# Attention by pairs of heads in alternating halves of TensorE's array, eight score buffers, division on VectorE

## The chip, the cores and the metric

The kernel runs on one core of a Trainium2 chip. Its engines work side by side and meet at semaphores: TensorE (PE, with its weight loads PEld), VectorE (DVE), ScalarE (ACT), GpSimd (POOL), and SyncE (SP), which issues most transfers. The metric is the device time of one execution in microseconds (us); lower is better.

## What is computed

Two transformer-like blocks over 512 tokens of width 1024. The first block (mixer, cross attention and feed-forward, twice) is not touched. The second block projects the tokens, runs an RWKV-7 state over eight heads, an attention over eight other heads, gates both and projects them out. The attention, of 8 heads of width 64, is what the change touches:

```python
def chunk_band_attention(q, k, v, q_g, k_g, rel_bias):
    ...
    s = jnp.einsum('bhnqd,bhnkd->bhnqk', qc, kb).astype(jnp.float32) * (HEAD_DIM ** -0.5)
    ...
    bias = rel_bias[:, rel_idx].astype(jnp.float32)
    ...
    s = s + bias[None, :, None]
    s = jnp.where(valid[None, None, :, None, :], s, -1e30)
    p = jax.nn.softmax(s, axis=-1).astype(v.dtype)
    o = jnp.einsum('bhnqk,bhnkd->bhnqd', p, vb)
    return o.reshape(b_, N_ATT_HEADS, s_, HEAD_DIM).transpose(0, 2, 1, 3).reshape(b_, s_, D_ATT)

# second_block
        y_a = chunk_band_attention(q, ka, va, q_norm_g[l], k_norm_g[l], rel_bias[l])
        y = jnp.concatenate([y_r * jax.nn.silu(g_r), y_a * jax.nn.silu(g_a)], axis=-1)
        x = x + gate[:, None, :] * (y @ w_out[l])
```

## The kernel before

**Products of weights.** Every large product is made of three matmuls of split operands (`mm3`, L324 to L326). ACT makes a weight chunk's high part (L298), VectorE its low part (L308), SP loads the chunks into three or four places in turn. `hi_to` and `lo_to` are where ACT and VectorE make the chunks due by then.

**Attention in tiles.** A tile k is one head h = k // 4 and 128 queries q = k % 4; causal, so it has 128 (q+1) keys. For each pair of tiles (k, k+1) of one head: TensorE makes the scores (`scores`, L1472; K is 64, so a matmul uses one half of the array's rows: heads with even number the first, odd ones the second); VectorE scales and adds the bias into a buffer `Sb[k % 4]` (L1534, L1535), takes the maximum of each tile (L1539), negates both (L1541), waits for ACT's exponentials of this pair (L1505) and takes the reciprocals of their sums (L1543); POOL divides (L1567); TensorE transposes the 128x128 pieces (`turned`, L1482); ACT copies them into `PTa[h % 2]` (L1513). When a head's four tiles are there, TensorE multiplies by the values (`values`, L1493, output in 64 of the 128 partitions of a bank), and VectorE gates (L1552). An fp32 matmul is two matmul instructions with a weight load each in the profile.

**The order.** `att_turns` writes the order out by hand, the same for each engine: in the step of pair n, first the values of a finished head, then `turned` for pair n-4, a yield, the scores of pair n, a yield. The yields interleave this with the dense products. `gemm_n` and `gemm_c` call `side()` after every six matmuls, through the stages `av` (attention's values) and `ag` (its gate); `late` is the generator of attention. The first scores come at the 15th of the 16 sides of `av`. The 16 sides of `ag` take attention up to `turned` of tiles 14 and 15. `closing` runs beside it in `ag`: it makes the diagonal for the output gate (VectorE L2348, TensorE L2327) and the gated RWKV rows (L2354, L2356).

**The tail.** Then `second_pe` and its like of the other engines run a loop of 18 turns. Each takes one step of attention; turns 1 to 8 add on TensorE one first part of the output product (`out_part_pe`, tokens t, row tiles 0 to 3, which hold the RWKV rows). Part (0,0) waits for the low half of those rows (`split_act` L2363, `split_dve` L2367, in turns 0 to 3 after that turn's step of attention). In turn 10, after the step of attention, ACT and VectorE make three weight chunks (`hi_to`, `lo_to`, n_out2 + 5). After the loop, attention's rows are split (L2439, L2457) and the output product goes on: parts 2 and 3 of each token tile, then the second half of the columns.

**The banks.** There are eight PSUM banks in a queue (`Banks`): `take` gives the one given back longest ago, and its new user waits until the old content was read (`vacant`). In the tail the output product holds four, so attention has the other four in turn.

## Time and profile before

| what | value |
| --- | --- |
| median of 3 runs | 1930.52 us (1925.89 to 1934.94) |
| the profiled execution's own time | 1928.67 us |
| its span, first to last instruction | 1926.8 us |
| TensorE busy | 1851.0 us, 96% |
| VectorE busy | 1028.7 us, 53% |
| ACT busy | 648.9 us, 34% |
| POOL busy | 172.2 us, 9% |
| mean granted TensorE clock | 0.983 of full |

The page's slices show TensorE's share of busy time and its granted clock along the span; the groups of instructions show what one instruction costs by shape; the chain that ended last shows which engine was waited for. Busy times of pipelined matmuls overlap, so the cost of a group on TensorE is read from the start of its first instruction to the start of the next group's first. The attention runs from 1775 to 1888 us of the span.

### The profile page before, as it was taken

How to read it: one execution, taken by the hardware profiler on the slowest of the kernel's cores; microseconds unless marked ns; L12 is line 12 of the kernel's file. 1: busy time of each engine (PE TensorE's matmuls, PEld its weight loads, DVE VectorE, ACT ScalarE, POOL GpSimd, SP SyncE). 2: the span in 40 equal slices, each digit the busy share in tenths (PEclk: the TensorE clock that was granted, in tenths of full speed). 3: DMA queues.
4: the chain of work that ended last, by engine and by line, in shares of the span. 5: the costliest groups of instructions: out<-in, count | busy, mean ns of one | idle time of the engine just before them, and what ended most of it. 6: DMA issues, size and time to landing. Idle time of an engine off the chain costs nothing.

```text
span 1926.8 us, 27348 instructions
## 1 busy us (share of the span) xinstructions
PE 1851.0 (96%) x11475; PEld 1529.8 (79%) x11475; DVE 1028.7 (53%) x1440; ACT 648.9 (34%) x999; POOL 172.2 (9%) x190
## 2 busy tenths in 40 slices
PE   7999999999999999999999999999989899998978
PEld 7879868888888898889868888878867787776546
DVE  4467347444454564446336556654566655445653
ACT  4332442323334322232432332334346232333441
POOL 3101001000000010001001000000020211111330
PEclk9999999999999999999999999999999999999998
DMA  8323323333323324332333545423232211114111
GB/s 269 113 88 109 99 66 99 120 93 94 98 88 121 98 90 119 98 110 99 99 105 122 155 149 164 143 88 99 77 109 61 59 57 35 46 35 143 41 37 44
DMA packets 145257, 189.65 MB, mean 98 GB/s; under 512 B 7688, under 2 KB 94980, under 8 KB 144240
## 3 DMA queue, kind: packets, MB, share of 16 engines
q1 hardware_dynamic: 139088, 168.32, 28.0%
q0 software_dynamic: 3488, 10.07, 1.6%
q10 hardware_dynamic: 2560, 9.53, 1.3%
q8 instruction: 91, 1.49, 0.3%
q14 instruction: 30, 0.25, 0.0%
HBM read 181.58 MB, written 6.30 MB: 98 GB/s over the span
## 4 chain that ended last, share of the span: by engine, by line
PE 87%; DVE 6%; issue 2%; ACT 2%; DMA 1%; POOL 1%; POOLq 0%; ACTq 0%; DVEq 0%
PE ps L324 25%; PE ps L325 24%; PE ps L326 24%; PE ps L2039 2%; PE ps L932 1%; PE ps L908 1%; PE ps L2025 1%; DVE WL L308 1%; PE ps L1472 1%; PE ps L2000 1%; ACT WH L298 1%; DMA RAW<-ab_w_in 1%; PE ps L509 1%; PE ps L2160 1%; PE ps L1493 1%
## 5 line engine op out<-in xcount | busy, mean ns | idle before, releaser
L308 DVE TENSOR_TENSOR WL<-RAW,WH 128x1024 fp32r<-128x1024 f32 x289 | 356.6, 1247 | 526.2 <-ACT WH L298 525.5
L324 PE MATMUL ps<-XH,WH 128*128 128x512 f32 (+1 forms) x1416 | 525.5, 371 | 3.9 <-DVE XL L522 3.5
L326 PE MATMUL ps<-XH,WL 128*128 128x512 f32 (+1 forms) x1416 | 519.2, 367 | 0.0
L325 PE MATMUL ps<-XL,WH 128*128 128x512 f32 (+1 forms) x1416 | 519.2, 367 | 0.0
L298 ACT ACTIVATE WH<-RAW 128x1024 fp32r<-128x1024 f32 x289 | 301.6, 1057 | 609.8 <-PE ps L326 577.9
L324 PE MATMUL ps<-WH,XH 128*128 128x512 f32 x800 | 322.4, 403 | 11.8 <-issue 4.2
L325 PE MATMUL ps<-WL,XH 128*128 128x512 f32 x800 | 315.4, 394 | 0.0
L326 PE MATMUL ps<-WH,XL 128*128 128x512 f32 x800 | 314.9, 394 | 0.0
L324 PEld LDWEIGHTS ps<-XH,WH 128*128 128x128 f32 x1416 | 268.8, 190 | 55.5 <-issue 9.3
L326 PEld LDWEIGHTS ps<-XH,WL 128*128 128x128 f32 x1416 | 268.5, 190 | 43.8
L325 PEld LDWEIGHTS ps<-XL,WH 128*128 128x128 f32 x1416 | 268.9, 190 | 41.5 <-issue 0.5
L324 PEld LDWEIGHTS ps<-WH,XH 128*128 128x128 f32 x800 | 152.2, 190 | 50.2 <-issue 9.2
L326 PEld LDWEIGHTS ps<-WH,XL 128*128 128x128 f32 x800 | 152.4, 191 | 32.6
L325 PEld LDWEIGHTS ps<-WL,XH 128*128 128x128 f32 x800 | 152.6, 191 | 30.1 <-issue 0.5
L648 POOL TENSOR_SCALAR SM<-SM 128x1 f32<-128x1 f32 x28 | 34.3, 1226 | 1201.0 <-DVE SM L636 1200.7
L516 ACT ACTIVATE XH<-ps 128x512 fp32r<-128x512 f32 x48 | 25.2, 604 | 142.3 <-PE ps L509 142.3
L1135 ACT ACTIVATE SCR<-SCR,VEC 128x512 f32<-128x512 f32 x44 | 31.9, 724 | 113.1 <-DVE SCR L1166 113.1
L1197 DVE TENSOR_TENSOR XL<-BIG,XH 128x512 fp32r<-128x512 f32 x88 | 56.1, 685 | 1.4 <-ACT XH L1189 1.4
L1189 ACT ACTIVATE XH<-BIG 128x512 fp32r<-128x512 f32 x88 | 49.4, 616 | 2.3 <-PE ps L326 2.3
L1169 DVE TENSOR_TENSOR BIG<-SCR,ps 128x512 f32<-128x512 f32 x44 | 30.3, 688 | 34.8 <-ACT SCR L1135 34.8
L2075 ACT ACTIVATE SCR<-ps 128x512 f32<-128x512 f32 x32 | 19.1, 597 | 85.8 <-PE ps L2039 85.8
L1567 POOL TENSOR_SCALAR LATE<-LATE,SM 128x128 f32<-128x128 f32 (+3 forms) x32 | 38.0, 1199 | 79.7 <-DVE SM L1543 79.7
(332 smaller groups left out, 1960.3 us busy)
## 6 DMA issues: line engine op xcount, KB each, us to landing
RAW<-ffn_w_up SPq DMA_DIRECT2D x176, 256.0 KB, 3.2
RAW<-ffn_w_down SPq DMA_DIRECT2D x44, 512.0 KB, 3.6
RAW<-w_in SPq DMA_DIRECT2D x33, 512.0 KB, 3.9
RAW<-xa_wkv SPq DMA_DIRECT2D x32, 512.0 KB, 4.0
RAW<-c_w_in SPq DMA_DIRECT2D x24, 512.0 KB, 3.7
LATE<-w_ada SPq DMA_DIRECT2D x24, 512.0 KB, 4.9
RAW<-xa_wq SPq DMA_DIRECT2D x16, 512.0 KB, 5.5
RAW<-xa_wo SPq DMA_DIRECT2D x16, 512.0 KB, 3.7
```

The costliest lines, as they stand in the source:

```text
L298: e.activation(halves_of(i)[0][:, :, 0:w], raw(i)[:, :, 0:w], ACT.Copy).then_inc(*w_hi.up(i))
L308: e.tensor_tensor(wl[:, :, 0:w], raw(i)[:, :, 0:w], wh[:, :, 0:w].bitcast(F), ALU.subtract).then_inc(*w_lo.up(i))
L324: e.matmul(o, lh, rh, start=start, stop=False)
L325: e.matmul(o, lh, rl, start=False, stop=False)
L326: return e.matmul(o, ll, rh, start=False, stop=stop)
L648: e.tensor_scalar(vr[:, t:t + 1], mv[:, t, 1:2], 1e-5, None, ALU.add).then_inc(*ln_g.up((n, t, "eps")))
L1135: e.activation(gc[i], gc[i], ACT.Gelu_apprx_tanh, bias=vec(f"fcb{l}", j)).then_inc(*ffn_a.up(("gelu", l, j)))
L1169: e.tensor_tensor(hT[:, j, :], c, ps.tile((("up", l, nb), i))[:, :], ALU.mult).then_inc(*ps.empties((("up", l, nb), i), ffn_v, ("h", l, j)))
L1189: e.activation(XH[:, kt % 8, :], hT[:, kt, :], ACT.Copy).then_inc(*x_hi.up(("h", l, j, kt)))
L1197: e.tensor_tensor(XL[:, kt % 8, :], hT[:, kt, :], XH[:, kt % 8, :].bitcast(F), ALU.subtract).then_inc(*x_lo.up(("h", l, j, kt)))
L1567: e.tensor_scalar(s, s, asum[:, n % 8 + j:n % 8 + j + 1], None, ALU.mult).then_inc(*at_g.up(k))
L2039: r = e.matmul(o, lhs[pps[cp], h, :], rhs[pps[cp], h, :], start=True, stop=True)
```

## The change

- Tiles are numbered anew (`att_of`): eight tiles k make a pair of heads; k % 2 is the head of the pair, k % 8 // 2 the queries q. A pair of tiles (n, n+1) is now two heads with the same q and the same number of keys.
- `scores` on TensorE cuts the keys in two and issues head a, head b, head a, head b, so that matmuls alternate between the halves of the array's rows. `values` runs over a pair of heads, alternating the halves of the array's columns, into one whole bank.
- There are eight score buffers, the four new ones in GB, which is free by then. `turned` comes for pair n-6, and `values` and the loop of the tail move with it: 20 turns instead of 18. The turns of the output parts and of `hi_to` and `lo_to` (10) stay.
- VectorE takes the maximum of both tiles in one instruction, with the negation in it, and a new step `normed` for pair n-2 after the scores of pair n: reciprocals, then the division of both tiles. POOL's part goes. The gating is one product of 128 partitions for each pair of heads.

```diff
@@ -1369,7 +1369,7 @@
     qTa, kTa = v4(B[4]), v4(L[3])
     xr = XR[:, :, :].rearrange("p a b -> p (a b)")
     PTa = [v4(xr[:, 2048 * i:2048 * i + 2048]) for i in range(2)]
-    Sb = [L[1][:, 512 * i:512 * i + 512] for i in range(4)]
+    Sb = [(L[1] if i < 4 else GB)[:, 512 * (i % 4):512 * (i % 4) + 512] for i in range(8)]
@@ -1441,134 +1441,138 @@
...
-    def att_turns(scores, turned, values):
+    def att_of(k):
+
+        return 2 * (k // 8) + k % 2, k % 8 // 2
+
+    def att_turns(scores, normed, turned, values):
 
         ready = []
-        for n in range(0, 36, 2):
-            for h in ready:
-                values(h)
+        for n in range(0, 38, 2):
+            for j in ready:
+                values(j)
             ready = []
-            for k in (n - 4, n - 3):
-                if k >= 0:
-                    turned(k)
-                    if k % 4 == 3:
-                        ready.append(k // 4)
+            if n >= 6:
+                turned(n - 6)
+                turned(n - 5)
+                if n % 8 == 4:
+                    ready.append(n // 8 - 1)
             yield
             if n < 32:
                 scores(n)
-            yield
-        for h in ready:
-            values(h)
+            if 2 <= n < 34:
+                normed(n - 2)
+            yield
+        for j in ready:
+            values(j)
+
+    def nothing(*args):
+        pass
 
     def att_pe_run(e):
         def scores(n):
-            h = n // 4
+            q, nk = att_of(n)[1], 64 * (att_of(n)[1] + 1)
             for k in (n, n + 1):
-                q, nk = k % 4, 128 * (k % 4 + 1)
-                b = ps.take(("as", k))
+                ps.take(("as", k))
                 for w in ps.vacant(("as", k)):
                     e.wait_ge(*w)
-                e.wait_ge(*at_v.at(("qk", 1, 3)))
-                e.matmul(b[:, 0:nk], qTa[halves(h), h // 2, 128 * q:128 * q + 128], kTa[halves(h), h // 2, 0:nk],
-                         start=True, stop=True).then_inc(*at_pe.up(("as", k)))
+            e.wait_ge(*at_v.at(("qk", 1, 3)))
+            for c in range(2):
+                for k in (n, n + 1):
+                    h = att_of(k)[0]
+                    r = e.matmul(ps.tile(("as", k))[:, nk * c:nk * c + nk], qTa[halves(h), h // 2, 128 * q:128 * q + 128],
+                                 kTa[halves(h), h // 2, nk * c:nk * c + nk], start=True, stop=True)
+                    if c:
+                        r.then_inc(*at_pe.up(("as", k)))
             ps.back(("as", n), ("as", n + 1))
 
         def turned(k):
             b = ps.take(("ap", k))
             for w in ps.vacant(("ap", k)):
                 e.wait_ge(*w)
-            e.wait_ge(*at_g.at(k))
-            for m in range(k % 4 + 1):
-                r = e.transpose(b[:, 128 * m:128 * m + 128], Sb[k % 4][:, 128 * m:128 * m + 128], ident)
+            e.wait_ge(*at_v.at(("p", k)))
+            for m in range(att_of(k)[1] + 1):
+                r = e.transpose(b[:, 128 * m:128 * m + 128], Sb[k % 8][:, 128 * m:128 * m + 128], ident)
             r.then_inc(*at_pe.up(("ap", k)))
             ps.back(("ap", k))
 
-        def values(h):
-            b = ps.take(("av", h))
-            for w in ps.vacant(("av", h)):
+        def values(j):
+            b = ps.take(("av", j))
+            for w in ps.vacant(("av", j)):
                 e.wait_ge(*w)
-            e.wait_ge(*at_a.at(("ap", 4 * h + 3)))
+            e.wait_ge(*at_a.at(("ap", 8 * j + 7)))
             e.wait_ge(*p2_a.at(("qkv", 2, 3)))
             for m in range(4):
-                r = e.matmul(b[halves(h), 128 * m:512], va[m][:, 64 * h:64 * h + 64], PTa[h % 2][:, m, 128 * m:512],
-                             start=m == 0, stop=m == 3)
-            r.then_inc(*at_pe.up(("av", h)))
-            ps.back(("av", h))
-        yield from att_turns(scores, turned, values)
+                for h in (2 * j, 2 * j + 1):
+                    r = e.matmul(b[halves(h), 128 * m:512], va[m][:, 64 * h:64 * h + 64], PTa[h % 2][:, m, 128 * m:512],
+                                 start=m == 0, stop=m == 3)
+            r.then_inc(*at_pe.up(("av", j)))
+            ps.back(("av", j))
+        yield from att_turns(scores, nothing, turned, values)
 
     def att_act_run(e):
         def scores(n):
             i = n % 8
             e.wait_ge(*at_v.at(("max", n)))
             for j, k in enumerate((n, n + 1)):
-                nk = 128 * (k % 4 + 1)
-                e.activation(Sb[k % 4][:, 0:nk], Sb[k % 4][:, 0:nk], ACT.Exp, bias=am[:, i + j:i + j + 1],
+                s = Sb[k % 8][:, 0:128 * (att_of(k)[1] + 1)]
+                e.activation(s, s, ACT.Exp, bias=am[:, i + j:i + j + 1],
                              accum_out=asum[:, i + j:i + j + 1]).then_inc(*at_a.up(("e", k)))
 
         def turned(k):
-            q, h = k % 4, k // 4
+            h, q = att_of(k)
             e.wait_ge(*at_pe.at(("ap", k)))
-            if h >= 2:
-                e.wait_ge(*at_pe.at(("av", h - 2)))
+            if k >= 8:
+                e.wait_ge(*at_pe.at(("av", k // 8 - 1)))
             e.activation(PTa[h % 2][:, 0:q + 1, 128 * q:128 * q + 128],
                          ps.tile(("ap", k))[:, 0:128 * (q + 1)].rearrange("p (m n) -> p m n", n=128),
                          ACT.Copy).then_inc(*ps.empties(("ap", k), at_a, ("ap", k)))
-
-        def values(h):
-            pass
-        yield from att_turns(scores, turned, values)
+        yield from att_turns(scores, nothing, turned, nothing)
 
     def att_dve_run(e):
         def scores(n):
-            h, i = n // 4, n % 8
+            i = n % 8
             for k in (n, n + 1):
-                nk = 128 * (k % 4 + 1)
-                lo, s, b = max(0, nk - 256), Sb[k % 4], ps.tile(("as", k))
+                h, q = att_of(k)
+                nk = 128 * (q + 1)
+                lo, s, b = max(0, nk - 256), Sb[k % 8], ps.tile(("as", k))
                 e.wait_ge(*at_pe.at(("as", k)))
                 if k < 4:
                     e.wait_ge(*p2_g.at("bias"))
                     e.wait_ge(*st_pe.at(("y", 7)))
+                elif k < 8:
+                    e.wait_ge(*st_v.at(("y", 7)))
                 else:
-                    e.wait_ge(*at_pe.at(("ap", k - 4)))
+                    e.wait_ge(*at_pe.at(("ap", k - 8)))
                 if lo:
                     e.tensor_scalar(s[:, 0:lo], b[:, 0:lo], 0.125, bias(h, 0, 1), ALU.mult, ALU.add).then_inc(*at_v.up())
                 e.scalar_tensor_tensor(out=s[:, lo:nk], in0=b[:, lo:nk], scalar=0.125, in1=bias(h, 256 - (nk - lo), 256),
                                        op0=ALU.mult, op1=ALU.add).then_inc(*ps.empties(("as", k), at_v, ("s", k)))
-            for j, k in enumerate((n, n + 1)):
-                e.wait_ge(*at_v.at(("s", k)))
-                e.tensor_reduce(am[:, i + j:i + j + 1], Sb[k % 4][:, 0:128 * (k % 4 + 1)], AX.X, ALU.max).then_inc(*at_v.up())
-            e.wait_ge(*latest["V"])
-            e.tensor_scalar(am[:, i:i + 2], am[:, i:i + 2], -1.0, None, ALU.mult).then_inc(*at_v.up(("max", n)))
+            s2 = (GB if n % 8 >= 4 else L[1]).rearrange("p (k m) -> p k m", k=4)[:, n % 4:n % 4 + 2, 0:128 * (att_of(n)[1] + 1)]
+            e.wait_ge(*at_v.at(("s", n + 1)))
+            e.tensor_reduce(am[:, i:i + 2], s2, AX.X, ALU.max, negate=True).then_inc(*at_v.up(("max", n)))
+
+        def normed(n):
+            i = n % 8
             e.wait_ge(*at_a.at(("e", n + 1)))
             e.reciprocal(asum[:, i:i + 2], asum[:, i:i + 2]).then_inc(*at_v.up(("sum", n)))
-
-        def turned(k):
-            pass
-
-        def values(h):
-            b, p = ps.tile(("av", h)), halves(h)
-            e.wait_ge(*at_pe.at(("av", h)))
-            e.wait_ge(*p2_v.at(("ag", h // 2)))
-            e.scalar_tensor_tensor(out=sga[h // 2][p, :], in0=sga[h // 2][p, :], scalar=0.5, in1=b[p, :], op0=ALU.mult,
-                                   op1=ALU.mult).then_inc(*ps.empties(("av", h), at_v, ("y", h)))
-        yield from att_turns(scores, turned, values)
+            e.wait_ge(*at_v.at(("sum", n)))
+            for j, k in enumerate((n, n + 1)):
+                s = Sb[k % 8][:, 0:128 * (att_of(k)[1] + 1)]
+                e.tensor_scalar(s, s, asum[:, i + j:i + j + 1], None, ALU.mult).then_inc(*at_v.up(("p", k)))
+
+        def values(j):
+            e.wait_ge(*at_pe.at(("av", j)))
+            e.wait_ge(*p2_v.at(("ag", j)))
+            e.scalar_tensor_tensor(out=sga[j], in0=sga[j], scalar=0.5, in1=ps.tile(("av", j))[:, :], op0=ALU.mult,
+                                   op1=ALU.mult).then_inc(*ps.empties(("av", j), at_v, ("y", j)))
+        yield from att_turns(scores, normed, nothing, values)
 
...
-
-    def att_pool_run(e):
-        def scores(n):
-            for j, k in enumerate((n, n + 1)):
-                s = Sb[k % 4][:, 0:128 * (k % 4 + 1)]
-                e.wait_ge(*at_v.at(("sum", n)))
-                e.tensor_scalar(s, s, asum[:, n % 8 + j:n % 8 + j + 1], None, ALU.mult).then_inc(*at_g.up(k))
-
-        def nothing(k):
-            pass
-        yield from att_turns(scores, nothing, nothing)
 
...
-        for n in range(18):
+        for n in range(20):
             next(late, None)
             if 1 <= n < 9:
                 out_part_pe(e, (n - 1) // 2, (n - 1) % 2)
@@ -2428,14 +2432,14 @@
...
-        for n in range(18):
+        for n in range(20):
             next(late, None)
             if n < 4:
                 split_act(e, n)
             if n == 10:
                 hi_to(e, n_out2 + 5)
         for m in range(4):
-            e.wait_ge(*at_v.at(("y", 2 * m + 1)))
+            e.wait_ge(*at_v.at(("y", m)))
             e.activation(XH[:, 4 + m, :], sga[m], ACT.Copy).then_inc(*x_hi.up(("y2", 4 + m)))
@@ -2446,7 +2450,7 @@
...
-        for n in range(18):
+        for n in range(20):
             next(late, None)
             if n < 4:
                 split_dve(e, n)
@@ -2467,10 +2471,8 @@
     def second_pool(e):
...
-        late = late_part(e, norm_qk_pool, att_pool_run)
+        late = norm_qk_pool(e, 1)
         dense_pool(e, rwkv(e, prep_own, tail_own, inverse_pool, state_turns, normed_pool), norm_qk_pool(e, 0), late, iter(()))
-        for n in range(18):
-            next(late, None)
 
     def out_part_pe(e, t, c):
```

## Rows read from the trace of the kernel before

**Rows 1.** The page, part 1: busy time (share) and instructions of each engine.

```profile
PE 1851.0 (96%) x11475; PEld 1529.8 (79%) x11475; DVE 1028.7 (53%) x1440; ACT 648.9 (34%) x999; POOL 172.2 (9%) x190
```

**Rows 2.** Windows: stretch, its length, busy time by engine, granted clock, DMA share, GB/s.

```profile
1775.27:1829.03 53.76, 49.45 (x213) 31.64 (x213) 35.43 (x88) 22.15 (x58) 20.62 (x16) 1.00 0.14 40
1829.03:1860.58 31.55, 28.28 (x112) 17.04 (x110) 16.15 (x44) 11.95 (x35) 10.31 (x10) 0.95 0.06 17
1860.58:1888.30 27.72, 17.20 (x53) 7.99 (x52) 13.30 (x27) 11.80 (x27) 7.06 (x6) 0.82 0.18 57
```

**Rows 3.** Timeline of TensorE, 1829 to 1842: start, us, engine, line, tiles, count.

```profile
1829.88 1.94 PE L1472 MATMUL ps<-LAST,BIG 64*128 64x384 f32 x4
1831.75 2.37 PE L1493 MATMUL ps<-XR,VL 128*64 128x512 f32 x8
1834.05 0.55 PE L1482 MATMUL ps<-CST,LATE 128*128 128x128 f32 x3
1837.87 0.77 PE L324 MATMUL ps<-WH,XH 128*128 128x512 f32 x1 [3.27 <-issue]
1838.43 0.63 PE L325 MATMUL ps<-WL,XH 128*128 128x512 f32 x1
...
1840.70 0.92 PE L1472 MATMUL ps<-LAST,BIG 64*128 64x128 f32 x4
1841.55 0.51 PE L324 MATMUL ps<-WH,XH 128*128 128x512 f32 x1
```

**Rows 4.** Timeline of TensorE, 1466 to 1468.6: L1796 between dense products.

```profile
1465.90 0.39 PE L325 MATMUL ps<-XL,WH 128*128 128x512 f32 x1
1466.13 0.39 PE L326 MATMUL ps<-XH,WL 128*128 128x512 f32 x1
1466.45 1.99 PE L1796 MATMUL ps<-LAST 64*128 64x512 f32 x8
1468.37 0.50 PE L324 MATMUL ps<-XH,WH 128*128 128x512 f32 x1
```

**Rows 5.** Timeline of TensorE, 1573.8 to 1577: first of L2180, and what follows.

```profile
1573.99 0.34 PE L2180 MATMUL ps<-BIG 64*64 64x64 f32 x4
...
1574.97 1.03 PE L2186 MATMUL ps<-RAW,LATE 64*64 64x64 f32 x15
```

**Rows 6.** Timeline of TensorE, 1564 to 1566.

```profile
1564.16 1.60 PE L2160 MATMUL ps<-GB,XR 64*128 64x64 f32 x16
```

**Rows 7.** Groups by shape, 1775 to 1889: xcount | busy, mean ns | idle before.

```profile
L1539 DVE TENSOR_REDUCE SM<-LATE 128x1 f32<-128x512 f32 x8 | 5.4, 677 | 0.0
...
L1541 DVE TENSOR_SCALAR SM<-SM 128x2 f32<-128x2 f32 x16 | 2.9, 181 | 0.6
...
L1552 DVE SCALAR_TENSOR_TENSOR RAW<-RAW,ps 64x512 f32<-64x512 f32 x4 | 2.7, 684 | 9.1 <-PE ps L1493 9.1
...
L1543 DVE RECIPROCAL SM<-SM 128x2 f32<-128x2 f32 x16 | 2.7, 166 | 20.3 <-ACT LATE L1505 20.3
...
L1539 DVE TENSOR_REDUCE SM<-LATE 128x1 f32<-128x128 f32 x8 | 2.2, 276 | 0.0
```

**Rows 8.** Lines L1161 and L1884 on VectorE: count, least/median/most ns of one.

```profile
L1161 DVE TENSOR_SCALAR SCR<-SCR,VEC x44: 479/481/484, 349.7 to 1297.4; 128x512 f32<-128x512 f32 x44
...
L1884 DVE TENSOR_SCALAR LAST<-GB,VEC x4: 275/278/4577, 1499.5 to 1504.4; 128x128 f32<-128x128 f32 x4
```

**Rows 9.** Waits of TensorE, 1775.2 to 1889: us in total, times, longest.

```profile
PE ps L2327 <- DVE SCR L2348: 2.2, 1, 2.2
PE ps L1482 <- DVE SM L1541: 2.0, 1, 2.0
```

**Rows 10.** Chain that ended last, 1860 to 1889: start, us, what.

```profile
1880.49 4.51 PE ps L1493 x8
...
1885.75 2.51 DVE XL L2457 x4
```

**Rows 11.** Timeline of VectorE, 1860 to 1892.

```profile
1867.72 3.71 DVE L308 TENSOR_TENSOR WL<-RAW,WH 128x1024 fp32r<-128x1024 f32 x3 [0.78 <-ACT WH L298]
```

## The prediction

> **What bounds the kernel now.** I read the page's first part first: TensorE is busy 1851 of 1926.8 us [rows 1], so outside a few places only less TensorE work makes this kernel shorter. The change touches only the second block's attention, so I cut that stretch out by stages [rows 2]. Stage A (53.8 us) runs from the first score pair to the last product of the dense stage; TensorE is busy 49.5 us of it. Stage B and C together (31.6 us) reach to the end of the eight first parts of the output product: the first of those parts starts at 1837.87 after a wait of 3.3 us [rows 3], which splits them into B (8.8 us) and C (22.7 us). Stage D (27.7 us) is the rest, up to where the output product goes on at 1888.30. In D TensorE is busy only 17.2 us and half of that is at the low clock (mean 0.82). What comes after D is output product on TensorE and stays as it is.
>
> So the question differs by stage. In A and C it is how much TensorE time attention takes. In B and D it is a chain: scores, VectorE, exponential, division, transposes, copy, values.
>
> The terms of attention on TensorE before, start to start: a score pair with 384 and 512 keys 1.87 us there (1829.88 to 1831.75; elsewhere 1.70), one with 128 and 256 keys 0.85 us (1840.70 to 1841.55), one head's values 2.30 us (1831.75 to 1834.05), one transpose about 0.11 us (three in 0.55, of which some 0.2 is the run-out of the last) [rows 3].
>
> **Part 1: two halves of the array in turn.** Nothing in attention before shows it, but other stages do. L1796 is of just this form: K of 64, heads' halves of the rows in turn, each into its own bank. Its eight instructions of 64x512 take 1466.45 to 1468.37, 1.92 us [rows 4]. In attention the same instructions in one half only cost (from the score pair: 4 instructions of mean 448 columns in 1.87 us less some 0.2 us for the change of form) 0.42 us each or 3.4 us for eight of 512 columns. So two halves in turn are twice as fast, 1.7 us plus 0.2. For values, L2180 and L2181 write column halves of one bank in turn: 32 instructions of 64 columns in 0.98 us (1573.99 to 1574.97), 0.031 us each [rows 5], where in one half 16 of this width cost 1.60 us, 0.10 each [rows 6]. I take half the time for both parts, the rest being 0.2 us a group.
> - Scores: both heads of a pair now have the same number of keys. By halves a pair takes (keys/128) x 0.21 + 0.2 us: 0.5 (taking more for the short one), 0.64, 0.85, 1.06 = 3.05 us for eight tiles, before 2 x (0.85+1.70) = 5.1. Over 32 tiles 8.2 us less.
> - Values: 4 x 2.3 instead of 8 x 2.3 us, 9.2 us less.
> - Transposes stay 80.
>
> One caution here is the number of weight loads: the scores are cut in two by keys, so a pair issues eight loads instead of four, of as little as 64 columns of stream each. With all loads in one half, 0.10 us each [rows 6] would put 0.8 us under every pair as its floor; L1796 shows loads of the two halves overlapping, so I leave 0.5 us. The Trainium skill (TensorE: Matmul & The Clock Gate, section LDWEIGHTS (loading the stationary operand)) says a load's time follows its columns, whatever K is, 107 ns for 128 of them. By that, without overlap, the two shorter pairs would cost 0.86 us each, 0.6 us more for eight tiles and 2.3 us more in all; the trace's 0.10 us agrees with its size.
>
> **Part 2: division on VectorE, and no wait for the exponential.** Before, each pair of tiles kept VectorE waiting for the exponential before its reciprocal: 20.3 us over 16 pairs [rows 7]. Now the division of pair n-2 comes after the scores of pair n, whose exponential is then long done. Added: 32 divisions by a column, SBUF to SBUF. 0.275 us at 128 columns and 0.481 at 512 [rows 8], evenly between: 8 x (0.28+0.35+0.41+0.48) = 12.2 us. Removed: 16 reductions (two tiles in one; the slope of 0.677 to 0.276 us over 384 columns leaves 0.14 us fixed each) 2.3 us, 16 negations 2.9 us, four of eight value products 2.7 us [rows 7]. Net 4.3 us more work and 20.3 us less waiting. POOL's 32 divisions, its only instructions in these stages [rows 2], go: 38.0 us, 2.4 a pair, leave the chain for 0.6 to 1.0 a pair.
>
> **Part 3: eight buffers, later turns.** Transposes of a pair come three steps after its scores, not two, so TensorE rarely waits for a division; two steps are added at the end. Buffers are no longer what scores wait for. Vector work and TensorE work can be up to two steps apart.
>
> **The schedule, stage by stage, times from the first score pair.** Stage A. TensorE before: 17 groups of six products at 1.37 us (0.23 each [rows 4]) 23.3; scores 5 x 0.85 + 4 x 1.70 = 11.1; 33 transposes 3.6; three heads' values 6.9; two gate products 2.0; waits for the diagonal (2.2) and for the buffer of tile 15 (2.0) [rows 9]; changes of form 2.7: 53.8. After: 23.3; nine pairs 6.6; 26 transposes 2.8; values of one pair of heads 2.3; 2.0; 2.4 for changes of form. That is 39.4, and about 1.7 of waits (the diagonal 0.8, a division 0.4, the rest where VectorE is just behind). 41.1 us, 12.7 less. VectorE does 35.4 us of work in this stage [rows 2]; with the additions 38 to 40 fall into 41, so it is nearly as full as TensorE, and ends it about 2 us behind.
>
> Stage B. The first output part waits for a row split that VectorE does after the scores of pair 18. Before: 8.8 us. After: six transposes and ACT's copies, gating (0.6 + 0.7), scores of 18 (256 keys, 1.3: two of 0.33 and one reduction of 0.65), one division pair hidden beside the exponential (1.1), split 0.6 and 0.8: first part at 6.9 us. 1.9 less. The wait in front of it grows from 3.3 to about 4 us, since the work that covered part of it (values 2.3 us, slower scores) is gone, so the low clock behind it stays: products 0.43 us apart instead of 0.23 [rows 3].
>
> Stage C. The same eight parts, four score pairs (0.85, 1.06, 0.5, 0.64), 14 tiles' transposes or so, one pair of heads' values, low clock for about 3 us: 20.7 us against 22.7. 2.0 less.
>
> Stage D. TensorE: transposes and scores 28 (2.0 us), VectorE to 3.9, exponential 5.5, then three weight splits that are queued there on ACT (2.9) and VectorE (3.7 [rows 11]): VectorE free at 10.2. Behind these on VectorE stands the gating product of values pair 2, and now something new: with four banks in turn, tile 31's scores take the bank of values pair 2, so TensorE's whole last score pair waits for that product, to 11.0. Before, it was issued ahead of the splits. Then at the low clock: scores 1.9, VectorE 2.1 more behind their start, exponential 1.6, division 0.17+0.48+0.4, transposes and copy 1.3, and values pair 3. Before, the last head's values took 4.51 us at the low clock [rows 10]; two heads by halves take the same: 23.8. Product 0.7 and four splits 2.5 [rows 10]: 27.1 us against 27.7. 0.6 less: what POOL and the exponential gave is taken by the late scores.
>
> **Sum.** 12.7+1.9+2.0+0.6 = 17.2, say 17.1 us. The profiled execution took 1928.67 us (span 1926.8 and 1.9 around it), 1.85 below the median of 1930.52. 1928.67 - 17.1 = 1911.6 us.
>
> **Bounds of the unknown.** Division: above, if it goes at the rate of one element (twice the slope: 0.28+0.41+0.55+0.68 us), 3.2 us more; below, it can't gain more than its 12.2 us, and half of that is covered. Halves: from no overlap (rival 2) to what I took. Clock in D: with the high clock for the last scores, transposes and values 4 to 5 us less.
>
> **Rivals.**
> 1. *VectorE becomes the bound in A and C.* Everything there that it does a little slower than added up delays TensorE after the two steps of slack. For it: 38 to 40 us of work in 41. Against: those durations are measured, and 20.3 us of wait go. With the slower division (3.2) and 0.1 us more at each of some 25 waits between dependent instructions: 5.7 us, 1917.3 us.
> 2. *The halves take turns and don't overlap* (the pairs then change nothing on TensorE). For it: these accumulate in one bank (values) and are cut short (scores). Against: rows 4 and 5. Price: A 5.0 (scores) + 2.3; B and C 2.3 + 2.3; D 0.6 + 1.7 + 4.3: 18.5 us. 1930.1 us, no change.
> 3. *Slower: the division is held on VectorE.* Of four divisions of this form at L1884 one took 4.58 us instead of 0.28 [rows 8]. If seven or more of 32 are so held in a full VectorE, 7 x 4.3 = 30 us stand in the chain: 1941.7 us. It decides from four (17 us) on. Against: none of the 44 at L1161 was held (479 to 484 ns) [rows 8].
> 4. *D at the high clock*: 1907 us.
>
> **Chances.** Forecast 0.66; rival 1 0.14; rival 2 0.11; rival 3 0.03; rival 4 0.06. The range reaches from below rival 4 to past rival 1: 1903 to 1923 us, leaving out rivals 2 and 3 and a few per cent at the ends. 0.5% is about what can be told from no change. Faster by over 0.5% (under 1920.9): forecast, rival 4, and most of rival 1: 0.83. Within 0.5%: rival 2 and the rest: 0.14. Slower: 0.03.
>
> **What would show it.** Eight score instructions of 256 columns in about 1.1 us and 16 of values in 2.3 to 2.5 us at the high clock (part 1); VectorE without a wait in front of its reciprocals and divisions of 0.28 to 0.48 us (part 2); stage A 41 us, the first output part 48 us after the first scores, its eight parts done at 69, the output product going on at 96; in D a wait of about 6 us in front of the last score pair that the product of values ends (part 3). The forecast is wrong if VectorE has no idle time in A, if score pairs keep 1.7 us, or if D is over 30 us.

## The result, and the profile after

| | before | changed |
| --- | --- | --- |
| median of 8 runs each | 1932.24 us (1925.89 to 1935.78) | 1921.37 us (1915.67 to 1923.81) |
| ratio | | 0.9945, 95% interval 0.993 to 0.9959 |
| profiled execution | 1928.67 us | 1917.38 us |
| its span | 1926.8 us | 1915.2 us |

The changed kernel is faster by about 10.6 us. The forecast was 17.1 us. The profiled spans differ by 11.6 us, but 1.4 of that lies ahead of the first attention scores, where both kernels run the same instructions: the scores start at 1773.89 us after and at 1775.27 before. In the thirteen profiles of this study that start lies anywhere from 1772.4 to 1779.8. So from here on I measure from the first score pair to where the output product goes on. That stretch went from 113.0 to 102.8 us; the forecast was 95.9.

The page's first part of the changed kernel, which answers to [rows 1], and its windows by stage, which answer to [rows 2] (the second window holds stages B and C):

```profile
PE 1835.1 (96%) x11539; PEld 1527.2 (80%) x11539; DVE 1030.1 (54%) x1436; ACT 649.3 (34%) x999; POOL 134.4 (7%) x158
```

```profile
1773.89:1817.36 43.47, 41.24 (x234) 29.93 (x234) 32.26 (x78) 20.41 (x56) 0.00 (x0) 0.96 0.16 49
1817.36:1848.30 30.94, 25.00 (x131) 17.50 (x130) 18.68 (x45) 12.40 (x36) 0.00 (x0) 0.83 0.06 18
1848.30:1876.68 28.38, 15.74 (x77) 9.48 (x75) 15.36 (x32) 12.73 (x29) 0.00 (x0) 0.70 0.18 56
```

TensorE has 15.9 us less work, POOL 37.8 us less. VectorE has 1.4 us more where 4.3 were expected. The granted clock is lower than before in every window (0.96, 0.83, 0.70 against 1.00, 0.95, 0.82): TensorE now has less to do, and waits more.

| stage, us | before | forecast | changed | missed by |
| --- | --- | --- | --- | --- |
| A | 53.8 | 41.1 | 43.5 | 2.4 |
| B | 8.8 | 6.9 | 9.4 | 2.5 |
| C | 22.7 | 20.7 | 21.5 | 0.8 |
| D | 27.7 | 27.1 | 28.4 | 1.3 |
| sum | 113.0 | 95.9 | 102.8 | 6.9 |

The forecast's four stages add up to 95.8; 95.9 is 113.0 less its 17.1.

TensorE's own work went as forecast. This is its timeline in the changed kernel (start, us, line, tiles, count, and the idle time before with what ended it), to be set beside [rows 3]:

```profile
1786.93 1.13 PE L1483 MATMUL ps<-LAST,BIG 64*128 64x256 f32 x8
...
1805.04 4.07 PE L1507 MATMUL ps<-XR,VL 128*64 128x512 f32 x16 [2.17 <-issue]
...
1821.43 0.72 PE L1483 MATMUL ps<-LAST,BIG 64*128 64x128 f32 x8 [3.25 <-DVE GB L1562]
1822.07 2.01 PE L1495 MATMUL ps<-CST,GB 128*128 128x128 f32 x8
1826.78 0.76 PE L324 MATMUL ps<-WH,XH 128*128 128x512 f32 x1 [2.69 <-issue]
1829.60 1.65 PE L1483 MATMUL ps<-LAST,BIG 64*128 64x192 f32 x8
1833.36 2.37 PE L1507 MATMUL ps<-XR,VL 128*64 128x512 f32 x16
1835.67 0.44 PE L1495 MATMUL ps<-CST,LATE 128*128 128x128 f32 x2
...
1858.99 2.08 PE L1483 MATMUL ps<-LAST,BIG 64*128 64x256 f32 x8 [5.68 <-DVE RAW L1567]
...
1868.96 4.53 PE L1507 MATMUL ps<-XR,VL 128*64 128x512 f32 x16 [0.73 <-ACT XR L1527]
1876.68 0.66 PE L324 MATMUL ps<-WH,XH 128*128 128x512 f32 x1 [3.19 <-DVE XL L2461]
```

A full score pair is 1.13 us and a pair of heads' values 2.31 us start to start (1833.36 to 1835.67). The wait of 5.68 us before the last score pair, ended by the gating product, stands where it was forecast. Three things are larger than forecast. The first values wait 2.17 us and then run at the low clock, 4.07 instead of 2.37 us. Score pair 18 waits 3.25 us and its successors run at the low clock. And the first output part waits another 2.69 us.

Who makes them wait? ScalarE's (ACT's) timeline in the changed kernel, around the first values and around score pair 18:

```profile
1798.78 0.60 ACT L1653 ACTIVATE LATE<-ps 128x512 f32<-128x512 f32 x1
1802.88 0.51 ACT L1519 ACTIVATE LATE<-LATE,SM 128x256 f32<-128x256 f32 x1 [3.51 <-DVE SM L1553]
...
1803.88 1.06 ACT L1527 ACTIVATE XR<-ps 128x512 f32<-128x512 f32 x2
1804.84 1.05 ACT L298 ACTIVATE WH<-RAW 128x1024 fp32r<-128x1024 f32 x1
...
1820.08 0.40 ACT L1519 ACTIVATE LATE<-LATE,SM 128x128 f32<-128x128 f32 x1 [2.15 <-DVE SM L1553]
...
1820.86 0.85 ACT L1527 ACTIVATE XR<-ps 128x384 f32<-128x384 f32 x2
```

And VectorE's, which made ACT wait:

```profile
1798.12 0.69 DVE L2358 TENSOR_TENSOR BIG<-BIG 128x512 f32<-128x512 f32 x1
...
1800.78 0.68 DVE L1662 SCALAR_TENSOR_TENSOR LATE<-LATE,ps 128x512 f32<-128x512 f32 x1
1801.38 0.75 DVE L1549 SCALAR_TENSOR_TENSOR LATE<-ps,VH 128x256 f32<-128x256 f32 x2
1802.16 0.69 DVE L1553 TENSOR_REDUCE SM<-LATE 128x2 f32<-128x512 f32 x1
...
1817.96 1.23 DVE L308 TENSOR_TENSOR WL<-RAW,WH 128x1024 fp32r<-128x1024 f32 x1 [2.21 <-ACT WH L298]
...
1819.62 0.42 DVE L1553 TENSOR_REDUCE SM<-LATE 128x2 f32<-128x256 f32 x1
```

The transposes of tiles 6 and 7 were done by 1799.0 (eight from 1797.95 on), but ACT copied them only at 1803.88. Its copies (L1527) stand in its queue behind the exponentials of pair 10 (L1519), and those wait 3.51 us for VectorE's maxima (L1553). VectorE is late there because the gated RWKV rows (L2358, L2360; four instructions, 1798.12 to 1800.8) and L1662 come first. The values wait for the copies. At 1820 the same happens again: ACT's copies stand behind exponential 16, that behind a reduction, and that behind a weight chunk (L308) for which VectorE waited 2.21 us on ACT (L298). Score pair 18 needs the bank that ACT's copy of tile 12 frees. TensorE's row puts this wait down to a division (L1562), but that one, of pair 14, is needed only by the transposes behind these scores; by the queue of banks, tile 19's scores take the bank of tile 12's transposes, and the copies that free it start at 1820.86.

So neither engine is full. In stage A VectorE is idle about 11 of 43.5 us, mostly waiting for ACT, and ACT waits 23 us for VectorE:

```profile
DVE WL L308 <- ACT WH L298: 6.0, 2, 3.6
DVE LATE L1549 <- PE ps L1483: 3.1, 2, 2.6
DVE LATE L1662 <- ACT LATE L1653: 2.4, 1, 2.4
```

```profile
ACT GB L1519 <- DVE SM L1553: 13.8, 4, 3.5
ACT LATE L1519 <- DVE SM L1553: 9.2, 4, 3.5
```

These are waits of the two engines in stage A of the changed kernel: us in total, times, longest. They are a ring of queues: reduction, exponential, then the copies and weight chunks behind it, then the next reductions. My theory after this reading: ACT's queue order costs the 4.9 us missed in A and B. The rivals are that TensorE's halves don't overlap as priced, or that VectorE is full.

### The profile page after: what moved, and what is told of

Its sections match the earlier page's. It is cut to its first block, busy times and chain, and to the rows that moved or that the text cites. A ratio compares the mean times of both kernels' runs of the same rounds, so it can differ in the third digit from the quotient of the medians.

```text
span 1915.2 us, 27416 instructions
## 1 busy us (share of the span) xinstructions
PE 1835.1 (96%) x11539; PEld 1527.2 (80%) x11539; DVE 1030.1 (54%) x1436; ACT 649.3 (34%) x999; POOL 134.4 (7%) x158
## 4 chain that ended last, share of the span: by engine, by line
PE 88%; DVE 6%; issue 2%; ACT 2%; DMA 1%; POOL 1%; ACTq 0%; DVEq 0%
PE ps L324 25%; PE ps L325 24%; PE ps L326 24%; PE ps L2043 2%; PE ps L932 2%; PE ps L908 1%; PE ps L2029 1%; DVE WL L308 1%; ACT WH L298 1%; PE ps L2004 1%; PE ps L1507 1%; PE ps L1483 1%; PE ps L2164 1%; DMA RAW<-xa_wkv 1%; PE ps L509 1%
## 5 line engine op out<-in xcount | busy, mean ns | idle before, releaser
L308 DVE TENSOR_TENSOR WL<-RAW,WH 128x1024 fp32r<-128x1024 f32 x289 | 356.4, 1246 | 528.4 <-ACT WH L298 527.4
L298 ACT ACTIVATE WH<-RAW 128x1024 fp32r<-128x1024 f32 x289 | 302.0, 1059 | 610.0 <-PE ps L326 573.8
L324 PE MATMUL ps<-WH,XH 128*128 128x512 f32 x800 | 322.6, 403 | 11.1 <-DVE XL L1197 3.7
L1135 ACT ACTIVATE SCR<-SCR,VEC 128x512 f32<-128x512 f32 x44 | 31.9, 725 | 113.0 <-DVE SCR L1166 113.0
L2128 DVE TENSOR_TENSOR SCR<-ps,GB 128x256 f32<-128x256 f32 x40 | 16.6, 423 | 47.1 <-PE ps L2029 46.5
```

The source lines that it names most:

```text
L298: e.activation(halves_of(i)[0][:, :, 0:w], raw(i)[:, :, 0:w], ACT.Copy).then_inc(*w_hi.up(i))
L308: e.tensor_tensor(wl[:, :, 0:w], raw(i)[:, :, 0:w], wh[:, :, 0:w].bitcast(F), ALU.subtract).then_inc(*w_lo.up(i))
L324: e.matmul(o, lh, rh, start=start, stop=False)
L1135: e.activation(gc[i], gc[i], ACT.Gelu_apprx_tanh, bias=vec(f"fcb{l}", j)).then_inc(*ffn_a.up(("gelu", l, j)))
```

## The experiments

Each kernel is the changed one with the edit shown. The stretch of the changed kernel is 102.8 us (102.6 in a second profile, below), its ratio to the kernel before 0.9945 (0.993 to 0.9959). Each ratio is to the kernel before on the same chip.

**The order within a pair.** The alternation of heads is undone in scores and values; head a's instructions all come before head b's.

```diff
-            for c in range(2):
-                for k in (n, n + 1):
+            for k in (n, n + 1):
+                for c in range(2):
...
-            for m in range(4):
-                for h in (2 * j, 2 * j + 1):
+            for h in (2 * j, 2 * j + 1):
+                for m in range(4):
```

> The changed kernel with the same matmuls in another order: each head's two score matmuls one after the other, and all four value matmuls of one head before the other's. Nothing else is moved. Stretch from the first score pair to where the output product goes on (changed kernel: 102.8 us in its profile). Theory (two halves in turn overlap and give about 17 us of TensorE time, some of it hidden in the waits of the last stage): score pairs of 512 keys take 1.9 us instead of 1.06, a values group 4.5 instead of 2.3, the stretch 114 to 119 us, the kernel 0.6 to 0.8% slower than the changed one, so about as fast as the kernel before. Rival (the order is worth little, the gain comes from the taken away waits): the stretch stays within 3 us of 102.8.

Measured: 1927.44 us, ratio 0.9961 (0.9946 to 0.9977); stretch 107.0 us. TensorE's timeline:

```profile
1838.46 3.93 PE L1507 MATMUL ps<-XR,VL 128*64 128x512 f32 x16
1842.32 0.44 PE L1495 MATMUL ps<-CST,LATE 128*128 128x128 f32 x2
...
1844.07 1.14 PE L1483 MATMUL ps<-LAST,BIG 64*128 64x256 f32 x8
```

The score pairs are as fast in series as alternated (1.14 against 1.13 us), though one after the other was expected to be slower. The values do lose: 3.86 us start to start against 2.31. Even that is less than twice the 2.30 us of one head [rows 3]. The stretch grows by 4.2 us where I expected over 11, and my rival within 3. In the totals this kernel can't be told from the changed one, as the intervals overlap. What was wrong in the expectation is that "in series" would mean "without overlap". The Trainium skill (TensorE: Matmul & The Clock Gate, section Part 3: Packing small matmuls — row/col tiling) says that matmuls keep program order in start and in end. By that, head b's first matmul would start no earlier than head a's fourth, and an ordered score pair would last clearly longer than an alternated one; the rows don't agree. My estimate of that: four instructions in one half take about 1 us (half of the 1.99 below); head b's would begin after three of head a's, 0.75 us in, and end at some 1.75 us. The score pair at 1791.45 in this kernel is followed by the next group at 1792.52, 1.07 us later, just as in the changed kernel; that reading doesn't rest on a profile's matmul ends, which are modelled.

**Are the scores' halves worth anything, and is the cut in the keys?** Two kernels. One has all score matmuls in the first half of the rows (odd heads' scores are computed from the other head's operands). The other doesn't cut the keys: four matmuls a pair, head a's two and then head b's.

```diff
-                    r = e.matmul(ps.tile(("as", k))[:, nk * c:nk * c + nk], qTa[halves(h), h // 2, 128 * q:128 * q + 128],
-                                 kTa[halves(h), h // 2, nk * c:nk * c + nk], start=True, stop=True)
+                    r = e.matmul(ps.tile(("as", k))[:, nk * c:nk * c + nk], qTa[0:64, h // 2, 128 * q:128 * q + 128],
+                                 kTa[0:64, h // 2, nk * c:nk * c + nk], start=True, stop=True)
```

> The changed kernel with both heads of a pair reading their queries and keys from the first 64 partitions, so that all eight score instructions of a pair use the same half of the array; the scores of odd heads are then not theirs (that part of the computation is changed). Same instructions, same sizes, same order. Theory (it is the two halves that overlap): a score pair of 512 keys takes 1.9 us instead of 1.06, one of 128 keys 0.8 instead of 0.55, and the stretch from first scores to output product grows by 4 to 8 us from 102.8. Rival (the four shorter instructions themselves run closer, whatever half they use, since the order made no difference in serial_both): 1.06 us stays.

```diff
-            for c in range(2):
-                for k in (n, n + 1):
...
+            for k in (n, n + 1):
+                h = att_of(k)[0]
+                e.matmul(ps.tile(("as", k))[:, 0:2 * nk], qTa[halves(h), h // 2, 128 * q:128 * q + 128],
+                         kTa[halves(h), h // 2, 0:2 * nk], start=True, stop=True).then_inc(*at_pe.up(("as", k)))
```

> The changed kernel with each head's scores in one matmul of all its keys, first one head, then the other: four instructions instead of eight in a pair. Theory (the halves run beside each other without being alternated, as serial_both's score pairs of 1.07 us show): a pair of 512 keys takes 1.0 to 1.3 us still, time as the changed kernel's within 0.2%. Rival (the second head can start only when the first one's last instruction has begun, and a half as large instruction leaves only half the overlap): 4 instructions of 0.43 us make 3 slots, 1.5 us for 512 keys, the stretch 2 to 3 us longer.

Measured: one half 1922.72 us (one execution), stretch 106.6; whole 1916.59 us, ratio 0.9919 (0.9896 to 0.9942), stretch 102.5. The full score pair in TensorE's timeline, first with all in one half, then uncut in two halves:

```profile
1790.23 1.99 PE L1483 MATMUL ps<-LAST,BIG 64*128 64x256 f32 x8
```

```profile
1786.90 1.13 PE L1482 MATMUL ps<-LAST,BIG 64*128 64x512 f32 x4
```

In one half a pair costs 1.99 us, in two 1.13. So the halves do overlap, and the gain comes from *pairing heads of different halves*, that is from `att_of`. Cutting the keys and alternating adds nothing for scores (its only trace is the shortest pair, 0.49 us uncut and 0.66 cut). The one-half kernel's stretch is 3.8 us longer than the changed one's, a little under the 4 to 8 expected; it rests on one execution.

**The copies ahead of the exponential on ACT.** Only ACT's order is changed: `turned` of a step before its `scores`' exponentials of the pair before.

```diff
-        yield from att_turns(scores, nothing, turned, nothing)
+        for n in range(0, 38, 2):
+            if n >= 6:
+                turned(n - 6)
+                turned(n - 5)
+            if 2 <= n < 34:
+                scores(n - 2)
+            yield
+            yield
```

> The changed kernel with ACT's order turned: in each turn it first copies the transposed tiles of pair n-6 and then makes the exponentials of pair n-2; in the changed kernel the exponentials of pair n came before the copies of pair n-4. Theory (the copies wait behind an exponential that waits for VectorE, and TensorE's values and scores wait for the copies): the waits of 2.2 us before the first values and of 3.3 us before score pair 18 go or fall below 1 us, the low clock in the first values (4.07 us) with them, and the stretch from first scores to output product falls from 102.8 to 96 to 99 us; faster than the changed kernel by 0.2 to 0.3%. Rival (VectorE is simply full, its lateness reaches TensorE by any way): the same two waits stay at 2 to 3 us in all, put down to VectorE.

Measured: 1913.49 us, ratio 0.99 (0.9872 to 0.9927); stretch 95.4. ACT's and TensorE's timelines:

```profile
1804.30 1.09 ACT L1527 ACTIVATE XR<-ps 128x512 f32<-128x512 f32 x2 [0.63 <-PE ps L1495]
1807.94 0.51 ACT L1519 ACTIVATE LATE<-LATE,SM 128x256 f32<-128x256 f32 x1 [2.55 <-DVE SM L1560]
...
1820.13 1.04 ACT L298 ACTIVATE WH<-RAW 128x1024 fp32r<-128x1024 f32 x1
```

```profile
1808.44 2.38 PE L1507 MATMUL ps<-XR,VL 128*64 128x512 f32 x16
...
1822.88 0.71 PE L1483 MATMUL ps<-LAST,BIG 64*128 64x128 f32 x8 [2.69 <-DVE LATE L1556]
```

And VectorE's, just before score pair 18:

```profile
1821.20 1.23 DVE L308 TENSOR_TENSOR WL<-RAW,WH 128x1024 fp32r<-128x1024 f32 x1 [1.68 <-ACT WH L298]
1822.34 0.48 DVE L1556 SCALAR_TENSOR_TENSOR LATE<-ps,VH 128x128 f32<-128x128 f32 x2
```

The copies shown at 1804.30 now wait only for the transposes, the first values start without a wait and at the high clock, and the first output part comes 48.3 us after the first scores. The forecast was 48.0, the changed kernel needs 52.9. Of the 7.4 us by which the stretch is shorter, 4.6 lie in A and B, the rest in C (1.1) and D (1.7). This shows that the place of the copies in ACT's queue cost stage A its 3.9 us. It does not show it for B. The stages are A 39.6, B 8.7, C 20.4 and D 26.7 us against 41.1, 6.9, 20.7 and 27.1 of the forecast: that the stretch is only 0.5 us off the forecast is luck, since A comes out 1.5 under and B 1.8 over. Score pair 18 still waits 2.69 us. Its first tile takes the bank that VectorE empties at 1822.34 (L1556), VectorE is late by the 1.68 us that it waits for a weight chunk of ACT (L298), and that chunk stands behind exponentials that wait for VectorE. So it is ACT's order again, but another instruction of it.

**VectorE's lateness alone.** The additions and gates of the RWKV rows, with the waits in front of them, are left out (the output lacks the bonus and the gate of these rows). ACT's order stays.

```diff
-                e.tensor_tensor(yT, yT, v4(B[3])[:, :, ts], ALU.add).then_inc(*nm_v.up(("bonus", t)))
...
-                e.scalar_tensor_tensor(out=yT, in0=yT, scalar=0.5, in1=v4(B[0])[:, :, ts], op0=ALU.mult,
-                                       op1=ALU.mult).then_inc(*nm_v.up(("yg", t)))
```

> The changed kernel without the bonus and the gate of the RWKV rows (eight instructions of 128x512 on VectorE, 5.3 us, in the second quarter of the gate stage); this part of the computation is left out. Theory (VectorE is late there, and ACT's exponentials and copies, queued behind it, are late for TensorE's first values): the wait of 2.2 us and the low clock in the first values go, 3 to 4 us less in stage A (43.5 us), the later waits stay. Rival (VectorE has slack in stage A, 11 us idle of 43.5, and its load does not matter): stage A stays within 1 us.

Measured: 1915.56 us, ratio 0.991 (0.9879 to 0.9941); stretch 99.7, A 40.1, B 11.1. The first values wait 0.69 instead of 2.17 us and run at the high clock. But score pair 18 waits 4.95 us instead of 3.25, so that the first output part comes at 51.2 against 52.9. Half of what A gains (3.4 us) is given back in B (1.7), since pair 18 waits for the same late copy. So VectorE's load does reach TensorE: with 5.3 us less of it the stretch is 3.1 us shorter. In the changed kernel it reaches TensorE's first values through ACT's queue, since with the copies first that wait is gone though this work is there.

**The chunks of the tail later.** ACT makes the three chunks in turn 17, VectorE in turn 14, after the gating product of values pair 2.

```diff
-            if n == 10:
+            if n == 17:
                 hi_to(e, n_out2 + 5)
...
-            if n == 10:
+            if n == 14:
                 lo_to(e, n_out2 + 5)
```

> The changed kernel with one thing moved: the three weight chunks that ACT and VectorE make in turn 10 of the tail are made in turn 17 (ACT) and 14 (VectorE). Theory (the product of values pair 2 stands behind them on VectorE, and TensorE's last score pair waits for its bank): the wait of 5.7 us in front of the last score pair goes down to under 2 us, the last stage from 28.4 us to 22 to 25, the kernel 0.2 to 0.3% faster than the changed one. Rival (the chunks are then made late and something else waits for them: the weights of the parts after, or the last values): the last stage shrinks by under 1 us, and a wait of TensorE for weights or for ACT's copies takes its place.

Measured: 1913.07 us, ratio 0.9902 (0.9877 to 0.9926); stretch 95.8, D 22.1 against 28.4. VectorE's timeline of the changed kernel around the last score pair, then TensorE's with the chunks later:

```profile
1854.80 3.50 DVE L308 TENSOR_TENSOR WL<-RAW,WH 128x1024 fp32r<-128x1024 f32 x3 [1.60 <-ACT WH L298]
1858.21 0.68 DVE L1567 SCALAR_TENSOR_TENSOR RAW<-RAW,ps 128x512 f32<-128x512 f32 x1
```

```profile
1854.15 1.14 PE L1483 MATMUL ps<-LAST,BIG 64*128 64x256 f32 x8 [0.59 <-DVE RAW L1567]
...
1858.75 1.07 PE L1495 MATMUL ps<-CST,GB 128*128 128x128 f32 x6 [2.88 <-DVE GB L1562]
```

The wait falls from 5.68 to 0.59 us, and the last score pair runs at the high clock (1.14 instead of 2.08 us). This shows the chain of stage D that the prediction gave. Its A and B are 41.8 and 11.1 us, and the first output part stands at 52.9 as in the changed kernel: whether the first values run at the low clock (4.07) or not (2.37, after a wait of 2.20 us) only moves time between A and B.

**The division back on POOL**, everything else as changed.

```diff
-                e.tensor_scalar(s, s, asum[:, i + j:i + j + 1], None, ALU.mult).then_inc(*at_v.up(("p", k)))
...
+                e.tensor_scalar(s, s, asum[:, i + j:i + j + 1], None, ALU.mult).then_inc(*at_g.up(("p", k)))
```

> The changed kernel with the division back on POOL, in the changed kernel's order (pair n-2 in turn n); VectorE only makes the reciprocals. Theory (division on VectorE costs it 12 us over the stretch, and VectorE's lateness sets the waits before the first values and before score pair 18; three turns of distance hide POOL's 1.5 to 2.8 us everywhere but at the end): stages A and B 2 to 4 us shorter than in the changed kernel (43.5 and 9.4 us), the last stage 2 to 3 us longer (POOL's last division 2.8 us instead of 1.0), time within 0.2% of the changed kernel. Rival (POOL's latency is what the move is for): A and B don't get shorter, the kernel is 0.2% or more slower than the changed one.

Measured: 1923.47 us, ratio 0.9958 (0.9943 to 0.9973); stretch 105.0, A 42.1, B 10.3, C 21.6, D 31.0. TensorE's waits in it: 

```profile
PE ps L1495 <- POOL GB L1573: 7.5, 7, 3.3
PE ps L1483 <- DVE RAW L1563: 5.7, 1, 5.7
```

TensorE waits 7.5 us for POOL, but its first values start without a wait, and A is even 1.4 us shorter: with less on VectorE, the reductions that ACT waits for seem to come earlier (argued, not tried alone). A and B together are 0.5 us shorter, where 2 to 4 were expected. D loses 2.6 us, where the division lies in the open. The move to VectorE is worth about 2.2 us of the stretch. In the totals the two can't be told apart (0.9958 against 0.9945, intervals overlap).

**Distance two.** Transposes for pair n-4 instead of n-6, eight buffers kept.

```diff
-        for n in range(0, 38, 2):
+        for n in range(0, 36, 2):
...
-            if n >= 6:
-                turned(n - 6)
-                turned(n - 5)
+            if n >= 4:
+                turned(n - 4)
+                turned(n - 3)
```

> The changed kernel with transposes two steps after their scores, as before the change, instead of three; 18 turns in all, eight buffers and all else kept. The values of pair 2 then come before the weight chunks of turn 10, and their product too. Theory (in the tail the third step costs: TensorE's last score pair waits behind the chunks; in stage A it covers waits for divisions): the wait of 5.7 us goes, the last stage is 22 to 26 us instead of 28.4, but TensorE waits for divisions in A, 1 to 3 us more; in all 0.1 to 0.3% faster than the changed kernel. Rival (VectorE is too late for two steps): A and C grow by more than 4 us, the kernel slower than the changed one.

Measured: 1925.71 us, ratio 0.998 (0.9963 to 0.9998); stretch 110.2. TensorE's waits in it:

```profile
PE ps L1495 <- DVE GB L1562: 12.4, 6, 5.5
PE ps L1495 <- DVE LATE L1562: 7.3, 6, 2.9
```

TensorE waits 19.7 us for divisions. My theory for this kernel fell and the rival held: undoing the third step of distance costs 7.4 of the 10.2 us that the change gained in the stretch.

**Together, and the changed kernel again.** Copies first and chunks later in one kernel; the same with each chunk of stage `ag` made at the start of its quarter, ahead of that quarter's first step of attention, by

```diff
+                if name == "ag":
+                    hi_to(e, min(first["in2", name] + c + 3, n_out2 + 3))
```

on ACT and `lo_to` likewise on VectorE; and the changed kernel a second time on that chip.

> The changed kernel with ACT's copies before its exponentials (copy_first) and the three weight chunks made after the last scores (late_split), together. Alone they took the stretch from 102.8 to 95.4 and 95.8 us. Theory (they cure different waits, the first ones in stages A and B, the last one in D): together 89 to 92 us, 0.984 to 0.989 of the kernel before. Rival (both only spare the same low clock, and the second has little left to spare): 94 us or more, not under 0.989.

> The same with a third thing moved: in the gate stage ACT and VectorE make the weight chunk due in a quarter at its start, before that quarter's first step of attention, and not after its second. Theory (what is left of the wait before score pair 18, 2.7 us in copy_first, is VectorE waiting 1.7 us for a weight chunk that ACT makes behind the exponentials): that wait falls below 1.5 us, the stretch is 1 to 3 us shorter than in copy_first_late_split. Rival (the chunk's place makes ACT's exponentials late instead): no gain or a loss of up to 2 us, with longer waits for divisions in A.

> The changed kernel itself, beside the next two on one chip, so that these are read against it. From its own runs: 0.9945 of the kernel before, between 0.992 and 0.996; stretch from first scores to output product 102.8 us, give or take 1.5 us by when the low clock falls.

| kernel | median, us | ratio (95%) | A | B | C | D | stretch |
| --- | --- | --- | --- | --- | --- | --- | --- |
| changed, again | 1920.42 | 0.9936 (0.9914 to 0.9957) | 43.4 | 9.5 | 21.4 | 28.4 | 102.6 |
| copies first, chunks later | 1907.18 | 0.9871 (0.9853 to 0.9889) | 39.6 | 8.7 | 20.5 | 22.0 | 90.8 |
| all three | 1907.13 | 0.9878 (0.9858 to 0.9897) | 40.8 | 6.3 | 20.9 | 22.1 | 90.0 |

The two gains mostly add up (7.4 and 7.0 alone, 12.0 of these 14.4 together in the stretch), and the result is faster than both kernels of this case: 25 us under the kernel before. The third edit does what it was for, score pair 18 waits 0.51 instead of 2.69 us. B falls from 8.7 to 6.3 us, against 6.9 in the forecast: this shows the cause that copies first left open in B. But 1.2 us of it is given back in A, where TensorE now waits for VectorE's diagonal, the stretch is only 0.8 us shorter where 1 to 3 were expected, and the time is the same:

```profile
1788.48 1.13 PE L2342 MATMUL ps<-SCR 128*128 128x128 f32 x8 [1.23 <-DVE SCR L2363]
...
1821.31 0.71 PE L1483 MATMUL ps<-LAST,BIG 64*128 64x128 f32 x8 [0.51 <-DVE SM L1565]
```

## Why the prediction was right, and where it was off

- **Direction and range: right.** Faster by 0.55% (0.41 to 0.7), 1921.4 us in a range of 1903 to 1923, near its upper end. Against the forecast's 17.1 us the runs give 10.6.
- **Part 1, halves: right.** Score pairs take 0.59, 0.65, 0.85 and 1.07 us start to start (0.66, 0.71, 0.92 and 1.13 busy) against 0.5, 0.64, 0.85 and 1.06; values 2.31 against 2.3. Rival 2 (the halves take turns) is false. Its price of 18.5 us is that of no overlap at all; the order alone is worth 4.2 us, and the rows put it in the values, since the score pairs are as fast. The caution about short weight loads shows only in the pair with 128 keys, 0.09 us over the forecast and 0.17 busy over the uncut pair.
- **Part 2, division: size right, worth overrated.** Divisions take 0.48, 0.62, 0.75 and 0.89 us for two, against 0.56 to 0.96 as costed. None was held (rival 3). Of the 20.3 us of waits before reciprocals 0.7 are left, though VectorE now waits more elsewhere, 9.9 us for ACT's weight chunks. But with the third step of distance most of POOL's chain is covered too, so the move is worth 2.2 us.
- **Part 3, distance: right, and a large part.** Undoing the third step costs 7.4 us. The halves cost about as much in two kernels: 3.8 us with the scores in one half, 4.2 with the values one head after the other. Added up with the division's 2.2 us these make 17.6, far more than the 10.2 gained: what a part costs when it alone is taken away is not its share of the gain (I take it that each part hides waits that another one leaves). The eight buffers and the merged maximum were not tried alone.
- **Stages A and B: the step that failed.** It is the term "about 1.7 of waits" in A, with B's "wait grows to about 4 us". I followed TensorE's and VectorE's queues, and took ACT's copies to come once the transposes were done: the sum has no term for ACT's queue. There they stand behind an exponential that waits for VectorE. Measured in A: 2.17 us of wait and 1.7 us of low clock in the values, 3.9 in place of 1.7, which is nearly the 2.4 missed. In B: waits of 3.25 and 2.69 us, 5.9 in place of 4, of which the first, before score pair 18, was not foreseen at all; and a further 1 us for transposes at the low clock (2.01 against 1.06). With the copies first A falls to 39.6 us, but B only to 8.7. B comes to 6.3 once ACT's weight chunk is also moved ahead.
- **VectorE: "nearly as full as TensorE" was wrong.** It does 32.3 us of work in A, not 38 to 40, and waits for the rest, mostly for ACT. Rival 1, VectorE as the bound, gave nearly the measured time (1917.3 against a profiled 1917.4), but by luck: its slower divisions (3.2 us) aren't there, and nothing shows its 0.1 us at each of 25 waits. What is true in it is that VectorE's lateness reaches TensorE, through ACT's queue.
- **Stage C.** 0.8 us over; the score pair at 1829.60 ran at the low clock (1.65 instead of 0.92 us).
- **Stage D: right.** The wait behind the three weight chunks is 5.68 us against "about 6", the values after it 4.53 against 4.5, the whole 28.4 against 27.1. (The steps that the prediction lists up to the end of the values add up to about 23.5 us; it says 23.8.) Rival 4, the high clock there, did not come by itself; making the chunks later brought it, and 6.3 us.

What stays open is why a wait of 2.2 us in front of the first values is followed by the low clock in one kernel and not in another (4.07 after 2.17 us, 2.37 after 2.20 us).

## What to carry to other kernels

When one engine is made faster, walk the queue of *every* engine in the chain in its new order, the nearly idle ones first: an instruction that is ready stands behind one that isn't, whatever the engine's busy share. Put what the bottleneck waits for (copies out of banks) ahead of what waits for another engine (exponentials). Then price the parts of a change apart: here the distance between producer and consumer and the two halves of the array carried about as much each, and the move between engines little.

## What the runs showed of the hardware

- Matmuls of two heads in the two halves of the rows ran side by side even when all of one head's were issued first: 1.14 us for 4 + 4 matmuls of 64x256, 1.13 for 2 + 2 of 64x512 and for eight alternated, 1.99 when all were in one half (busy times; start to start 1.07, 1.05, 1.07 and 1.92). For values (column halves, 8 + 8 matmuls) this holds only in part: 3.86 us in series, 2.31 alternated, 4.6 for two heads before. So here alternation mattered for the values and not for the scores; whether that is due to the length of the series or to rows against columns was not tried.
- The low clock was seen after long waits. After TensorE waited 5.68 us, eight score matmuls took 2.08 us and the values, after further waits, 4.53; the granted clock was 0.50 in both stretches, the lower of the two levels (1.2 GHz). At 1786.93 and 1833.36, with a granted clock of 1.00 (2.4 GHz), the same took 1.13 and 2.37; factors 1.84 and 1.91. So a wait costs more than itself: D fell by 6.3 us when 5.1 us of wait went, though other waits in D grew by some 1.3 us in all (a division's from 2.42 to 2.88).
